# Key loads and first finish loads spread over the steps, the end of the second attention stage reordered, and GpSimd in place of VectorE for some low halves of weight tiles

## The reference

```python
h = rmsnorm(x) * (1 + scale) + shift                 # scale, shift, gate from silu(c) @ w_ada + b_ada
qa, ka, va, za, qb, kb, vb, zb, ga, gb = split(h @ w_in)
oa = neighbourhood_attention(qa, ka, va, cache_a)     # 8 heads of 64, window 8 x 16, 512 cached keys
ob = window_attention(rope(qb), rope(kb), vb, cache_b, sink)   # 8 query heads, 2 key heads, +-128 tokens
ya = (oa * silu(za)) @ w_br_a
yb = (ob * silu(zb)) @ w_br_b
m = sigmoid(ga) * ya + sigmoid(gb) * yb
y = rmsnorm(x + gate * (m @ w_out)) * final_norm_g
```

## Time and profile before

| | |
|---|---|
| runs | 1131.45, 1132.85, 1133.99 us; median 1132.85 us |
| profiled execution | 1132.45 us, of which 1130.6 us from its first to its last instruction |
| PE busy | 1078.7 us, 95% of the span |
| mean granted TensorE clock | 0.986 |
| DVE, ACT, POOL busy | 68%, 55%, 9% |

### The profile page before, as it was taken

The page is one execution under the profiler, slowest core; times in us unless marked ns, Lnnn a source line. Parts: engine busy times, 40 slices in busy tenths (PEclk is TensorE's granted clock), DMA queues, the critical chain, the costliest instruction groups (busy, mean ns, idle before and its releaser), DMA issues.

```text
span 1130.6 us, 18385 instructions
## 1 busy us (share of the span) xinstructions
PE 1078.7 (95%) x6459; PEld 958.7 (85%) x6459; DVE 774.5 (68%) x1535; ACT 624.4 (55%) x1126; POOL 103.0 (9%) x115
## 2 busy tenths in 40 slices
PE   7899999999999999997999999899989599999997
PEld 1799888989989998896888888788868599898896
DVE  6869678767757876774777777688669475445443
ACT  6842347735645763664576576577468454344342
POOL 0000200000000000000000000000000154343430
PEclk9999999999999999998999999999999799999999
DMA  9825538965892985699289299399289985443630
GB/s 359 320 86 142 180 102 164 182 173 106 183 219 62 192 170 144 136 186 254 57 186 190 65 180 198 106 184 175 81 197 181 232 293 187 140 167 111 204 130 38
DMA packets 318975, 188.34 MB, mean 167 GB/s; under 512 B 256166, under 2 KB 297766, under 8 KB 318892
## 3 DMA queue, kind: packets, MB, share of 16 engines
q1 hardware_dynamic: 305068, 165.31, 60.0%
q10 hardware_dynamic: 13824, 21.96, 6.2%
HBM read 94.27 MB, written 32.12 MB: 112 GB/s over the span
## 4 chain that ended last, share of the span: by engine, by line
PE 73%; DVE 8%; DMA 6%; SPq 4%; ACT 4%; issue 3%; ACTq 0%; POOL 0%; DVEq 0%
PE d_ps_pairs L94 19%; PE s_ps_pairs L94 13%; PE b_ps L94 10%; PE y_ps L2131 10%; PE o_ps_pairs L1046 6%; PE v_ps L94 5%; DMA xl<-pl 4%; PE s_ps_pairs L1217 3%; PE s_ps_pairs L1218 3%; SPq L1135 3%; DVE pl L1688 2%; DVE mn L1611 2%; DMA x<-in_w_ada 2%; ACT pr L1359 2%; ACT ph L1379 1%
## 5 line engine op out<-in xcount | busy, mean ns | idle before, releaser
L94 PE MATMUL d_ps_pairs<-h,wt 128*128 128x384 f32 (+4 forms) x1848 | 349.0, 344 | 0.1
L94 PEld LDWEIGHTS d_ps_pairs<-h,wt 128*128 128x128 f32 x1848 | 319.9, 188 | 14.8 <-DVE wt L1700 1.4
L94 PE MATMUL s_ps_pairs<-h,wt 128*128 128x512 f32 (+1 forms) x864 | 172.9, 358 | 0.0
L94 PEld LDWEIGHTS s_ps_pairs<-h,wt 128*128 128x128 f32 x864 | 143.1, 191 | 22.0
L1688 DVE SCALAR_TENSOR_TENSOR pl<-pr,rden,ph 128x896 f16<-128x896 f32 (+1 forms) x128 | 140.4, 1116 | 30.5 <-DMA xl<-pl 23.1
L1359 ACT ACTIVATE pr<-s_ps_pairs,mx 128x896 f32<-128x896 f32 (+1 forms) x128 | 124.7, 978 | 64.6 <-DVE mx L1633 64.4
L1379 ACT ACTIVATE ph<-pr,rden 128x896 f16<-128x896 f32 (+1 forms) x128 | 125.1, 1011 | 10.4 <-DVE rden L1669 5.9
L2131 PE MATMUL y_ps<-wo,mg 128*128 128x512 f32 (+1 forms) x504 | 113.3, 385 | 0.0
L2131 PEld LDWEIGHTS y_ps<-wo,mg 128*128 128x128 f32 x504 | 91.4, 188 | 20.5
L1611 DVE TENSOR_REDUCE mn<-s_ps_pairs 128x2 f32<-128x1024 f32 x64 | 78.2, 1222 | 32.3 <-PE s_ps_pairs L1218 31.9
L94 PE MATMUL b_ps<-og,wb 128*128 128x256 f32 x720 | 89.4, 286 | 6.1 <-DVE tp L2210 6.1
(11 more groups left out here) (236 smaller groups left out, 1627.1 us busy)
## 6 DMA issues: line engine op xcount, KB each, us to landing
wraw<-in_w_gate SPq DMA_DIRECT2D x24, 512.0 KB, 4.3
gt<-gates_d SPq DMA_DIRECT2D x40, 256.0 KB, 4.1
wada<-in_w_ada SPq DMA_DIRECT2D x12, 512.0 KB, 7.2
gates_d<-craw ACTq DMA_DIRECT2D x30, 192.0 KB, 3.0
oz<-gates_d SPq DMA_DIRECT2D x20, 256.0 KB, 4.3
oz<-o_d SPq DMA_DIRECT2D x20, 256.0 KB, 3.9
x_f<-in_x SPq DMA_DIRECT2D x10, 512.0 KB, 6.3
y<-y_f SPq DMA_DIRECT2D x9, 512.0 KB, 2.7
```

The costliest lines, as they stand in the source:

```text
L94: mm = eng.matmul(out, lhs(a, k), rhs(b, k), start=(k == 0 and i == 0), stop=(k == n_k - 1 and i == 2))
```

## The change

1. `kb_d` gets a third part, so that it holds high, low, high. Each of the two rows of 64 partitions of a head's keys can then come in one transfer of 128 partitions. front stores two more blocks of 327 KB (`kb_d<-kst` six times where it was four), and everything that waits for front's stores waits for these too.
2. The keys are loaded in pieces. In stage A's last pair head 0's keys are loaded after the turns of step 5 (655 KB), the prompt columns of head 1 after step 6 (131 KB), its latent columns after the last turn (524 KB). In stage B's pair 1 the prompt columns of both heads are loaded after step 6, the rest after the last turn. The latter have a semaphore of their own, which PE waits for at the scores of step 1 and not of step 0.
3. In the last pair the loads of `load_first` come apart: gates and sums 0, 1, 2 behind the turns of steps 1, 2, 3 with gate 3, the sums 3 at step 6, and the first two `gt` after step 7. All four SiLUs stand at ACT's step 4 (three stood at step 3 and one behind the loop), the four `first_gated` at DVE's steps 5 to 8. The first store of `o_d` moves ahead of the exponentials of step 6. The two `x_f` weights are issued from ACT's queue behind the loop and no longer from SP's ahead of the last turns. `low_half` and `add_halves` of the last three steps move into finish, among the sigmoids, `tile_high_f` and `tile_low_f` of its first chunk. On PE the weighted sum of step 7 moves ahead of `branch(0, 1)`; `branch(0, 0)` waits for one weight tile less.
4. GpSimd makes the low halves of the weight tiles of stage B's first three pairs (4 each), which DVE made at L1700.
5. `mg` and `tp` become two tensors each, of the same size together.

```diff
@@ -350,9 +350,9 @@
...
-                for part in range(2):
+                for at in range(3):
                     for kv in range(2):
-                        sp.dma_start(io["kb_d"][kv, part], kst[kv * HD:(kv + 1) * HD, part, :].bitcast(F32)
+                        sp.dma_start(io["kb_d"][kv, at], kst[kv * HD:(kv + 1) * HD, at % 2, :].bitcast(F32)
@@ -833,7 +833,7 @@
...
-    return [(v_out[i], 16 * 2 * TT // 4) for i in range(4)] + [(out_done, 192), (v_max, 2 * TT + 3)], (v_hi, v_max)
+    return [(v_out[i], 16 * 2 * TT // 4) for i in range(4)] + [(out_done, 224), (v_max, 2 * TT + 3)], (v_hi, v_max)
@@ -1104,13 +1141,11 @@
...
 
-            def load_keys(kv, steps):
-
-                sp.wait_ge(s_done, steps)
-                for h in range(2):
-                    for part in range(2):
-                        r0 = HD * ((h + part) % 2)
-                        sp.dma_start(kk[r0:r0 + HD, h, :].bitcast(F32), io["kb_d"][kv, part]).then_inc(kk_in, 16)
+            def load_keys(kv, h, c0, c1, done):
+
+                sp.dma_start(kk[:, h, c0:c1].bitcast(F32), io["kb_d"][kv, h:h + 2, :, c0:c1].rearrange("a d t -> (a d) t")
+                             ).then_inc(done, 16)
+
@@ -1135,31 +1170,46 @@
                     sp.dma_start_transpose(halves(part, n)[:, t, 0:k, :], src[:, t, 0:k * P]).then_inc(landed[t], 16)
 
             for s in range(STEPS):
-                if s == STEPS - 1 and not A and not last and fresh(p + 1):
-                    load_keys((p + 1) // 2, (pb + 1) * STEPS)
-                if s == STEPS - 1 and A and p == PAIRS - 1:
-                    load_keys(0, (pb + 1) * STEPS)
-                if s == STEPS - 1 and last:
-                    sp.wait_ge(s_done, (pb + 1) * STEPS)
-                    load_weight(sp, f, io, 2)
-                    load_weight(sp, f, io, 3)
                 if BEHIND:
                     turn(s, 0)
                 for n in range(1, len(SPLITS)):
                     if split_at(n - 1, p) + 1 == s:
                         load_tile(n)
+                if not BEHIND:
+                    turn(s, 0)
+                turn(s, 1)
+                if A and p == PAIRS - 1 and s == 5:
+                    load_keys(0, 0, 0, TOK, kk_in[0])
+                if A and p == PAIRS - 1 and s == 6:
+                    load_keys(0, 1, LAT, TOK, kk_in[0])
+                if not A and p == 1 and s == 6:
+                    load_keys(1, 0, LAT, TOK, kk_in[0])
+                    load_keys(1, 1, LAT, TOK, kk_in[0])
                 if last and s == 1:
                     sp.wait_ge(x_used, p * NG + NG)
                     sp.wait_ge(o_out_a, PAIRS * 16)
                     sp.wait_ge(o_out, p * 32)
-                    for n in range(3):
-                        load_first(sp, f, io, n)
+                if last and 1 <= s < 4:
+                    load_first_gate(sp, f, io, s - 1)
+                    load_first_sums(sp, f, io, s - 1)
+                if last and s == 3:
+                    load_first_gate(sp, f, io, 3)
+                if last and s == 6:
+                    sp.wait_ge(o_out, p * 32 + 16)
+                    load_first_sums(sp, f, io, 3)
                 if last and s == 7:
-                    sp.wait_ge(o_out, p * 32 + 16)
-                    load_first(sp, f, io, 3)
-                if not BEHIND:
-                    turn(s, 0)
-                turn(s, 1)
+                    sp.wait_ge(m_done, (pb + 1) * 2 * STEPS)
+                    for slot in range(2):
+                        sp.wait_ge(g_out[slot], in_slot(slot, UNIT0[pb]) * 16)
+                    load_gt(sp, f, io, 0, 0)
+                    load_gt(sp, f, io, 0, 1)
+            if A and p == PAIRS - 1:
+                sp.wait_ge(s_done, (pb + 1) * STEPS)
+                load_keys(0, 1, 0, LAT, kk_in[1])
+            if not A and p == 1:
+                sp.wait_ge(s_done, (pb + 1) * STEPS)
+                load_keys(1, 0, 0, LAT, kk_in[1])
+                load_keys(1, 1, 0, LAT, kk_in[1])
 
         turns(sp, body)
 
@@ -1172,6 +1222,16 @@
                 r1 = HD * (1 - h)
                 pool.memset(q2[r1:r1 + HD, h, :].bitcast(F32), 0.0).then_inc(q2_zero, 1)
                 pool.wait_ge(q2_zero, h + 1)
+
+    if not A:
+        @block.gpsimd
+        def _(pool):
+            for p in range(PAIRS - 1):
+                for n in range(len(SPLITS)):
+                    i = SPLITS[n][0]
+                    pool.wait_ge(w_hi, p * TILES + BEFORE + n + 1)
+                    pool.tensor_tensor(wt[:, SLOT[i], 1, :], wraw[:, :], wt[:, SLOT[i], 0, :].bitcast(F32), ALU.subtract
+                                       ).then_inc(w_lo, 1)
 
     @block.tensor
     def _(pe):
@@ -1223,13 +1283,14 @@
...
-                        pe.wait_ge(kk_in, (p // 2 + 1) * 64)
+                        pe.wait_ge(kk_in[0], (p // 2 + 1) * 32)
...
                     if s == 1 and not A:
                         pe.wait_ge(r_raw, p * NG + NG)
+                        pe.wait_ge(kk_in[1], 48 if p > 1 else 16)
@@ -1445,7 +1496,10 @@
             ahead = p < PAIRS - 1
             for s in range(STEPS):
                 if s >= 2 + BEHIND:
-                    low_half(s - 2 - BEHIND)
+                    low_half(act, p, s - 2 - BEHIND)
+                if last and s == 6:
+                    act.wait_ge(o_done, pb * STEPS + 3)
+                    act.dma_start(io["o_d"][pb, :, 0:2 * P], ost[:, 0:2 * P]).then_inc(o_out, 16)
                 if s > 0:
                     exps(s)
                 upper(s)
@@ -1455,33 +1509,27 @@
                 gate(s + UNITS_AHEAD)
                 gate_out(s + UNITS_AHEAD)
                 tile_highs(s)
-                if last and s == 6:
-                    act.wait_ge(o_done, pb * STEPS + 3)
-                    act.dma_start(io["o_d"][pb, :, 0:2 * P], ost[:, 0:2 * P]).then_inc(o_out, 16)
-                if last and s == 3:
-                    for n in range(3):
+                if last and s == 4:
+                    for n in range(PIECES):
                         first_silu(act, f, n)
             if A and not ahead:
                 gate(STEPS)
                 gate_out(STEPS)
+            if last:
+                act.wait_ge(s_done, (pb + 1) * STEPS)
+                load_weight(act, f, io, 2)
+                load_weight(act, f, io, 3)
+                return
             if BEHIND:
-                low_half(STEPS - 3)
-            if last:
-                first_silu(act, f, 3)
+                low_half(act, p, STEPS - 3)
             if ahead:
                 projected(0, p + 1)
-            low_half(STEPS - 2)
-            if not last:
-                tile_highs(STEPS)
+            low_half(act, p, STEPS - 2)
+            tile_highs(STEPS)
             if not A:
                 act.wait_ge(o_done, pb * STEPS + STEPS - 1)
-                t0 = 2 * P if last else 0
-                act.dma_start(io["o_d"][pb, :, t0:LAT - P], ost[:, t0:LAT - P]).then_inc(o_out, 16)
-            if last:
-                act.wait_ge(d_done, UNIT0[pb + 1])
-                tile_high_f(act, f, 2)
-                tile_high_f(act, f, 3)
-            low_half(STEPS - 1)
+                act.dma_start(io["o_d"][pb, :, 0:LAT - P], ost[:, 0:LAT - P]).then_inc(o_out, 16)
+            low_half(act, p, STEPS - 1)
             act.wait_ge(o_done, (pb + 1) * STEPS)
             t0 = 0 if A else LAT - P
             act.dma_start(io["o_d"][pb, :, t0:TOK], ost[:, t0:TOK]).then_inc(o_out, 16)
@@ -1703,32 +1751,8 @@
...
                 for n in range(len(SPLITS)):
-                    if split_at(n, p) == s:
+                    if split_at(n, p) == s and (A or last):
                         tile_low(n)
-
@@ -1771,27 +1795,24 @@
...
-                    first_gated(dve, f, s - 3)
+                        add_halves(dve, p, s - 3)
+                if last and s >= 5:
+                    first_gated(dve, f, s - 5)
             if BEHIND:
                 lower(STEPS - 1)
             tile_lows(STEPS - 1)
+            if last:
@@ -1853,6 +1885,7 @@
...
     dve.wait_ge(f["silu_done"], n + 1)
+    dve.wait_ge(f["first_in"][n], 32)
@@ -1945,26 +1981,20 @@
...
+            load_gt(sp, f, io, i, j)
 
         sp.wait_ge(w_lo, TILES_TOTAL)
         load_w(4)
-        sp.wait_ge(m_done, ALL * 2 * STEPS)
-        for slot in range(2):
-            sp.wait_ge(g_out[slot], in_slot(slot, UNIT0[ALL - 1]) * 16)
-        load_gt(0, 0)
-        load_gt(0, 1)
         for slot in range(2):
             sp.wait_ge(g_out[slot], in_slot(slot, UNIT0[ALL]) * 16)
         load_w(5)
         sp.wait_ge(pv_done, ALL * STEPS)
-        load_gt(0, 2)
-        load_gt(0, 3)
+        load_gate(0, 2)
+        load_gate(0, 3)
         load_w(6)
         sp.wait_ge(o_out, PAIRS * 32 + 16)
 
@@ -2028,11 +2058,22 @@
...
 
+        low_half(act, PAIRS - 1, STEPS - 3)
+        low_half(act, PAIRS - 1, STEPS - 2)
+        sigmoid(0, 0)
+        sigmoid(0, 1)
+        act.wait_ge(d_done, UNIT0[ALL])
```

(40 more changed lines are left out.)

153 lines of the change are left out of this document (84 added, 69 removed).

## The result

The changed kernel takes 1136.55 us (median of 20 runs, 1132.51 to 1145.67), the kernel before 1133.38 (median of 20, 1131.14 to 1135.33). The ratio is 1.0031, 95% interval 1.0019 to 1.0042: slower by 0.3%, where 1112.8 us and a gain were forecast. The runs of the changed kernel also spread over 13.2 us, those before over 4.2. The profiled execution took 1139.04 us, 2.5 more than the median, with a span of 1137.2.

The account below looks back on a forecast made before the run. PE was taken as the bound, with only its waits and lower-clock time to win. Terms 1.0 - 6.3 - 4.9 - 4.0 - 7.9 + 2.0 = -20.1 from 1132.85 gave 1112.8 us, range 1104 to 1124.

Parts of the forecast that it names:

- What bounds the kernel: Whole kernel: PE busy 1078.7 of 1130.6 us; only its idle time and lower-clock time can be won.
- Front: Before stage A: two more stores of 327 KB, awaited by all engines, cost +1.0 us, between 0 and 1.9.
- Stage A to B: Join of the stages: 6.33-us gap and slow clock mostly go, less delayed turns; -6.3 us, from -8.7 to -2.5.
- Pair 1 to 2: Stage B's join of these pairs: 3.89-us gap plus 1.7 of slow clock to win; -4.9 us, from -5.6 to -3.
- The last pair: Stage B's last pair: spread loads win 7.1 us, the SiLU block returns 3.1; -4.0 us, from -7 to -1.
- Three SiLUs stood there already at 4.2 us: Last pair: the new four-SiLU block is only 0.6 us longer and may start up to 3 us late.
- The end of stage B and finish: Scores of step 8 to the branches' end: 42.1 us against 50.0, so -7.9 us, from -10.7 to -3.
- it moves by about 0.8, to +18.8: Finish: the last `xl` turn lands 0.8 us earlier, 18.8 us after the scores of step 8 start.
- GpSimd: Stage B's first three pairs: moving 12 low halves to it costs +2.0 us, between -1.4 and +5.1.
- at the others VectorE is in its reduction or its `pl`: Nine tiles not meeting `nm`: VectorE has 1.4 us or more idle in the step; no cost charged.
- GpSimd's lock is on the path nearly each time: Rival, chance 0.04: each of 12 operations delays `nm` by its whole 2.4 us, 29 us in all; 1139.8 us, slower.
- point of decision: In the GpSimd lock rival: the cost per operation from which it decides, 22.1 / 12 = 1.84 us.

Follow-up runs that it names:

- e3_both: Changed kernel with VectorE making the low halves again and the x_f weights issued from SP ahead of the last turns: 1125.73 us, ratio 0.9925 to the kernel before.
- e1_dve_lows: Changed kernel with VectorE, not GpSimd, making the low halves of stage B's weight tiles in all pairs: 1128.11 us, ratio 0.9950 to the kernel before.
- e2_xf_sp: Changed kernel with the two x_f weights issued from SP ahead of the turns of step 8 again: 1136.09 us, ratio 1.0022 to the kernel before.
- e5_xf_act_early: Changed kernel with VectorE's low halves back and the x_f weights on ScalarE's queue, issued ahead of its last ph: 1123.75 us, ratio 0.9913.
- e6_xf_behind: Changed kernel with VectorE's low halves back and the x_f weights on SP behind the last turns: 1122.74 us, ratio 0.9911 to the kernel before.
- e4_before_pool: Kernel before with one part alone, GpSimd making the 12 low halves in pairs 0 to 2 of stage B: 1143.71 us, ratio 1.0088.
- e9_keys_behind: e3_both with all key loads behind the last turns, none after steps 5 and 6: 1128.77 us, ratio 0.9964 to the kernel before.

## Why the prediction was wrong, by its own steps

**What bounds the kernel** was right, and so was the aim: the three gaps are gone or smaller. The kernel before hid other things in them and in the low clock behind them.

**Front**, +1.0: measured +1.3, between +0.7 and +4.4 in the ten traces.

**Stage A to B**, -6.3: measured -4.0. The gap is 2.21 us, and a new one of 1.13 us stands at 512.9, at the sum whose turns meet the 655 KB. The clock fell again, which the term had at nothing: 0.12 x 12.9 = 1.5 us, by the first of these rows of the changed kernel (table by stretch, as the earlier trace rows; each stretch begins where PE's gap ends). The size was off, inside its bounds. Part of it is the execution: of the ten traces with these same instructions, four stayed at 1.00 here (behind gaps of 1.97 to 2.37 us) and six fell to 0.87 or 0.88 (behind 2.06 to 2.53 us).

```profile
527.11:540.00 12.89, 12.89 (x62) 10.56 (x63) 6.50 (x15) 5.32 (x16) 0.00 (x0) 0.88 0.81 278
731.58:742.00 10.42, 10.42 (x49) 10.23 (x50) 7.16 (x21) 6.32 (x12) 2.39 (x1) 0.84 0.60 143
857.88:870.00 12.12, 12.12 (x67) 11.24 (x68) 10.94 (x25) 8.92 (x16) 1.57 (x2) 0.86 0.72 138
901.56:920.00 18.44, 15.19 (x108) 14.06 (x108) 9.44 (x14) 9.42 (x14) 7.10 (x7) 0.89 0.72 263
```

The first of these places in e3_both:

```profile
527.26:540.00 12.74, 12.74 (x68) 10.78 (x69) 6.21 (x14) 5.41 (x17) 0.00 (x0) 1.00 0.86 284
```

**Pair 1 to 2**, -4.9: measured -5.5, and then 2.1 us come back at the next place where PE waits, the gate's copy behind the rotation of the queries. In both kernels that chain of ScalarE and VectorE takes its 20 us from the last sum of pair 1 (709.65 to 729.95 before, 704.16 to 725.04 in e3_both). Before, PE was busy for all these 20.3 us at a mean clock of 0.92, a loss of 1.6 us, and came out just as the chain did. Now it runs them at 1.00, is done after 18.9 us and waits the rest. So the 1.7 us of low clock that the prediction counted as a gain could not be won: the chain takes its 20 us either way. With 1.2 us at the keys' own step the term is -2.2, and -2.2 by e1_dve_lows too, whose pairs 0 to 2 run from 561.93 to 782.68 where before it was 565.98 to 788.89. Behind the new wait the changed kernel's clock fell as well (0.84 over 10.4 us, the second row: 1.7 us). In e3_both it stayed at 1.00 behind a gap of about the same length, 1.95 us, and so it did in five of the twelve traces with the keys loaded this way or later; what decides that is open. What the stalled PE left time for was not listed in the prediction.

**The last pair**, -4.0: measured -0.6. The mechanism was named and its size not: 3.1 us were charged, and it was 4.1 us of gap, 0.14 x 12.1 = 1.7 us of lower clock (third row), and 0.7 us at step 8 (a gap of 1.00 where it was 0.34), 6.5 of the 7.1 won. The prediction took the three SiLUs of the kernel before as a cost that was there already ("Three SiLUs stood there already at 4.2 us"). They cost nothing: in that kernel they ran while everything behind was late by the 4.94-us gap anyway, and PE waited 0.15 us for the exponentials behind them.

**The end of stage B and finish**, -7.9: measured +2.8, and -1.8 with the x_f weights on SP (e2_xf_sp: the shift goes from +4.0 to +2.2). Here a step failed in kind. The prediction said of the last turn that "it moves by about 0.8, to +18.8": it counted issue times and left the landing at 4.7 us, whatever bytes stand ahead of the turns or beside them. In the changed kernel the x_f weights run beside the turns, from another queue (changed kernel, the DMA issues, then one stretch of the table by stretch with DMA share and GB/s last):

```profile
x_f<-in_w_br ACTq DMA_DIRECT2D x2, 512.0 KB, 11.7
...
xh<-ph SPq DMA_TRANSPOSE x2, 13.9
...
xl<-pl SPq DMA_TRANSPOSE x2, 10.1
```

```profile
890.00:894.00 4.00, 0.01 (x1) 0.00 (x0) 0.76 (x2) 1.06 (x2) 0.72 (x1) 0.75 1.03 84
```

The turns took 13.9 and 10.1 us against 6.3 and 4.1 before (medians of two each, issues from 880 to 887 us; the 5.4 and 4.7 in the expectation of e2_xf_sp are those of the second `xh` and the first `xl`), and the weights 11.7 against 5.9. The last sum starts at +27.5, not at +18.8; in e3_both too it starts at +22.9. Behind the gap the clock is 0.89 over 18.4 us (fourth row above), a loss of 2.0 us, and the branches take 22.8 us from 903.93 to 926.70, about what was charged (17.2 + 4.5). Where the weights keep clear of the turns most of the forecast comes: from the scores of step 8 to the first product of the output projection it is 49.8 us before, 52.6 in the changed kernel, 48.1 in e3_both, 45.2 in e5_xf_act_early and 44.6 in e6_xf_behind, 5.2 us less than before where 7.9 were forecast.

**GpSimd**, +2.0: by whole runs +9 to +10 (e1_dve_lows, e4_before_pool), outside its bounds (+5.1). By the traces, the changed kernel against e1_dve_lows, the same three pairs are 3.6, 3.3 and 2.4 us longer, together 9.2. This is the largest miss together with finish, and it alone turns the sign: without it the change is a gain (0.9950). What the prediction said of `nm` was right: three tiles meet it in e4_before_pool, as forecast, and cost PE 2.27, 1.05 and 1.05 us where 2.3, 1.4 and 1.4 were charged. What failed is the step that put the other nine at nothing: "at the others VectorE is in its reduction or its `pl`". Being at `pl` was the collision. In nine of the 12 cases of the changed kernel a `pl` is started or queued while GpSimd's operation runs, and `pl` has both inputs in SBUF; it becomes 0.5 to 2.1 us longer. The idle 1.4 us of VectorE come after `pl`, ahead of the next reduction, and don't help ScalarE, which waits for `pl` in between.

The Trainium skill's rule ("SBUF — State Buffer", section SBUF: two separate sides), that a VectorE operation with two SBUF inputs and a GpSimd operation exclude each other, is borne out by the 3.28 us above, by the 2.35 us of `nm`, and the other way round by GpSimd's 3.13 us behind a `pl`. The rival that was built on it, "GpSimd's lock is on the path nearly each time", had 0.04 and was right in kind: 0.8 us an operation, not 2.4, but with the other terms worth only 6 us and not 22, 0.8 was enough. Its point of decision was worked out as 1.84 us from terms that were too large. (Its text also says 8.9 us where its own figures, 29 - 22.1, give 6.9; the 1139.8 us go by 6.9. And the -3 at the bad end of finish is -3.6 by the figures beside it.)

Sum of the terms in the profile: 1.3 - 4.0 - 2.2 + 9.2 - 0.6 + 2.8 = +6.5, the +6.6 of the spans but for rounding. The medians are 3.2 us apart; the profiled execution of the changed kernel lay 2.5 above its median.

## What to carry to other kernels

Before a stall is counted as a gain, list what the other engines do during it: here a block of SiLUs, a rotation chain and late loads stood in the gaps and in the low clock behind them, and came out as waits when these went. Before elementwise work is moved to GpSimd, look at what VectorE has in its queue at the moment when GpSimd's input gets ready, and who waits for that; free time of VectorE elsewhere doesn't count. A bulk load is costed by what stands behind it and beside it on the transfer engines, not by the queue that issues it. And a term read from one trace is laid beside other traces of the same instructions, where there are any: here they differ by 2 us and more.

## What the runs showed of the hardware

The transfer engines' busy share says little of what they deliver: from 890 to 894 us of the changed kernel they were busy at 1.03 with 84 GB/s, with weights from one queue and turns from another (the stretch shown above); the kernel before moved 210 GB/s at 1.16 from 884 to 890 us:

```profile
884.00:890.00 6.00, 3.85 (x18) 3.85 (x19) 0.72 (x2) 0.00 (x0) 1.26 (x1) 0.58 1.16 210
```

An operation of VectorE on 128x2 elements, 0.16 us, takes 2.35 us when GpSimd's started 0.07 us before it, both with their inputs in SBUF; the custom operation, which has one input in PSUM and one in SBUF, is not held (0.62 us, started 0.19 us behind GpSimd's).

Gaps of PE of about 2 us were followed by the lower clock in one execution and by full clock in another: 1.90 us by 0.84 over 10.4 us, 1.95 us by 1.00; and in ten traces of the same instructions at one place six fell and four did not, with gap lengths that overlap.

The changed kernel scattered more (13.2 us in 20 runs) than e3_both (2.2 us in 5), but this doesn't go with the x_f weights or the collisions: e9_keys_behind, with neither, spread over 8.8 us in 12 runs, and e4_before_pool, with the collisions, over 2.2 in 5. What makes it is open.
